# A second buffer for the raw up-projection weights of a two-layer encoder, and a new placement of its SBUF buffers

## What is computed

```python
def conv_ffn(h, w_up, conv_w, conv_b, w_down):
    u = h @ w_up                                   # 1024 -> 2 * 2816
    y = conv_b
    for j in range(CONV_WIDTH):                    # causal depthwise, width 3
        y = y + conv_w[j] * _shift(u, CONV_WIDTH - 1 - j)
    a, g = jnp.split(y, 2, axis=-1)
    return (jax.nn.silu(g) * a) @ w_down           # 2816 -> 1024
...
    h = h + m @ w_out[i]
    h = h + conv_ffn(rmsnorm(h, ffn_norm_g[i]), w_up[i], conv_w[i], conv_b[i], w_down[i])
```

## Time and profile before

| | us |
|---|---|
| median of 3 runs | 2754.95 |
| lowest, highest | 2752.99, 2756.72 |
| the profiled execution | 2758.29 |
| its span, first to last recorded instruction | 2756.5 |

### The profile page before, as it was taken

The page is one execution under the profiler, slowest core; times in us unless marked ns, Lnnn a source line. Parts: engine busy times, 40 slices in busy tenths (PEclk is TensorE's granted clock), DMA queues, the critical chain, the costliest instruction groups (busy, mean ns, idle before and its releaser), DMA issues. The chain is left out here.

```text
span 2756.5 us, 40721 instructions
## 1 busy us (share of the span) xinstructions
PE 2610.5 (95%) x14038; PEld 2265.8 (82%) x14038; DVE 1557.0 (56%) x2684; ACT 1267.7 (46%) x2809; POOL 1512.9 (55%) x1083
## 2 busy tenths in 40 slices
PE   7799899999879999999899999999988999999999
PEld 6599788888668888888789999989866888888877
DVE  5899777741755565555541114656238555555645
ACT  5687666641433333333345546767224333333332
POOL 2034433203667777767755443555138776777773
PEclk9899999999899999999999999999989999999999
DMA  5100000101011121111131111333101111111212
GB/s 177 46 24 24 28 9 6 69 24 39 31 38 54 49 67 51 46 46 61 46 119 47 50 43 28 87 90 108 63 31 41 51 46 46 52 55 49 65 38 92
DMA packets 77352, 147.16 MB, mean 53 GB/s; under 512 B 8528, under 2 KB 45568, under 8 KB 75552
## 3 DMA queue, kind: packets, MB, share of 16 engines
q1 hardware_dynamic: 77216, 145.38, 16.1%
HBM read 122.22 MB, written 13.69 MB: 49 GB/s over the span
## 5 line engine op out<-in xcount | busy, mean ns | idle before, releaser
L729 PE MATMUL banks<-XQH,WH 128*128 128x512 f32 x1120 | 441.9, 395 | 41.3 <-ACT U L450 26.4
L594 POOL TENSOR_TENSOR WL<-WR,WH 128x512 fp32r<-128x512 f32 x216 | 379.0, 1774 | 185.7 <-ACT WH L430 169.0
L729 PE MATMUL banks<-XQH,WL 128*128 128x512 f32 x1120 | 438.6, 392 | 0.0
L729 PE MATMUL banks<-XQL,WH 128*128 128x512 f32 x1120 | 438.5, 391 | 0.0
L855 DVE TENSOR_TENSOR XT<-XT,banks 128x1024 f32<-128x1024 f32 x176 | 214.3, 1218 | 180.6 <-PE banks L764 180.5
L729 PEld LDWEIGHTS banks<-XQH,WH 128*128 128x128 f32 x1120 | 212.0, 189 | 95.7 <-issue 29.9
L594 POOL TENSOR_TENSOR WL<-WF,WH 128x512 fp32r<-128x512 f32 x168 | 256.4, 1537 | 5.2 <-ACT WH L436 5.2
L729 PEld LDWEIGHTS banks<-XQL,WH 128*128 128x128 f32 x1120 | 211.9, 189 | 44.8
L729 PEld LDWEIGHTS banks<-XQH,WL 128*128 128x128 f32 x1120 | 212.2, 189 | 43.1
L839 DVE SCALAR_TENSOR_TENSOR YG<-U,CONVW,YG 128x1023 f32<-128x1023 f32 x88 | 170.1, 1933 | 95.9 <-ACT YG L474 95.8
L764 PE MATMUL banks<-AH,WH 128*128 128x512 f32 x640 | 197.6, 390 | 2.6 <-DVE XT L855 2.6
(11 more groups left out here) (326 smaller groups left out, 6577.3 us busy)
## 6 DMA issues: line engine op xcount, KB each, us to landing
WR<-in_up SPq DMA_DIRECT2D x88, 512.0 KB, 4.2
WF<-in_down SPq DMA_DIRECT2D x88, 256.0 KB, 2.6
HT<-HC SPq DMA_DIRECT2D x224, 64.0 KB, 2.0
QWR<-in_qkv SPq DMA_DIRECT2D x8, 1536.0 KB, 7.5
XT<-in_xT SPq DMA_DIRECT2D x16, 512.0 KB, 7.8
OWR<-in_w_o SPq DMA_DIRECT2D x16, 512.0 KB, 3.3
QWR1F<-in_qkv SPq DMA_DIRECT2D x4, 1536.0 KB, 6.3
spill<-XT SPq DMA_DIRECT2D x8, 512.0 KB, 11.2
```

The source lines that it names most:

```text
L594: pool.tensor_tensor(out_, src, hi.bitcast(F32), ALU.subtract).then_inc(signal, 1)
L729: mm = pe.matmul(BANK[bank], w[:, n, b * P:(b + 1) * P], x[:, b, :], start=(first and b == 0 and w is WH and x is XH[i]), stop=(b == 3 and ...
```

## The change

Two things are changed.

1. **Two raw buffers.** Even pairs are loaded into WR, odd pairs into a new tile `RAW_ODD` (WRB), each with its own semaphore. Pair p now waits for the low parts of pair p - 2. The first odd load waits until PE has summed the squares of the norm (`norm.summed`), since WRB takes the place of `ACC`, which that sum reads. SP's order changes: pairs 1, 2 and 3 are issued ahead of the loop, and in the loop the down weights come first, then pairs 4 and 5 (numbers of the first turn). ACT's wait ahead of `bias(pair, 0)` of pair 20 becomes a wait for pair 20's own low parts.
2. **Placement.** To find 8 KB, large buffers start at 384 modulo 512 bytes in place of 0, so that nothing is lost ahead of the first one; ROOTS, BITF and IDB share one row of 512 bytes that is later reused; CONVW and CONVB are packed; VAR lies in the last 64 bytes. Built, the buffers up to GAIN lie 128 bytes lower than before, those of the feed-forward part 640 bytes lower, ACC and QKVB 384 bytes higher. So all large buffers keep their distances modulo 512. WRB starts at 221056, WR at 102272, also equal modulo 512.

```diff
+PLACE = 384
...
     def row(self):
-        self.at = (self.at + ROW - 1) // ROW * ROW
+        self.at = (self.at - PLACE + ROW - 1) // ROW * ROW + PLACE
...
+    def landed(self):
+        return self.at(16, 32 * ((self.p + 1) // 2))
...
+        VAR = nc.alloc_sbuf_tensor_at(f"VAR{stage}", [P, TT], F32, offset=c.top - 64)
...
-        VAR = m.take(f"VAR{stage}", [P, TT], F32)
+        RAW_ODD = nc.alloc_sbuf_tensor_at(f"WRB{layer}", [P, 2, D], F32, offset=m.at)
...
-                sp.wait_ge(w_lo, CLASSIC if p == 1 else Pair(it, p - 1).end())
+                if p >= 2:
+                    sp.wait_ge(w_lo, CLASSIC * (p - 1) if p < 4 and it is None else Pair(it, p - 2).end())
                 for k in range(2):
-                    sp.dma_start(RAW[:, k, :], up[pair.tap(k)]).then_inc(raw_landed, 16)
+                    sp.dma_start((RAW, RAW_ODD)[p % 2][:, k, :], up[pair.tap(k)]).then_inc(raw_landed[p % 2], 16)
...
+            sp.wait_ge(norm.summed, 1)
             load_pair(None, 1)
+            load_pair(None, 2)
+            load_pair(None, 3)
             with sp.Fori(0, LOOPS) as it:
-                load_pair(it, 2)
                 load_down(it, 0)
-                load_pair(it, 3)
-            load_pair(None, LAST - 1)
-            load_pair(None, LAST)
+                load_pair(it, 4)
+                load_pair(it, 5)
...
-            act.wait_ge(w_lo, last.end())
+            act.wait_ge(w_lo, pair.end())
...
+        c.IDB = nc.alloc_sbuf_tensor_at("IDB", [P, P], BF16, offset=m.at)
+        c.ROOTS = nc.alloc_sbuf_tensor_at("ROOTS", [P, TT * DSA.nh], F32, offset=m.at + 2 * P)
+        c.BITF = nc.alloc_sbuf_tensor_at("BITF", [P, 17], F32, offset=m.at + 2 * P + roots)
```

More of the change, by code:

```diff
@@ L311, in ffn_phase @@
         AH = m.take(f"AH{layer}", [P, 2, S], F32R)
[L312 removed]
+        RAW_ODD = nc.alloc_sbuf_tensor_at(f"WRB{layer}", [P, 2, D], F32, offset=m.at)
+        m.at += 2 * 4 * D
+        assert m.at <= c.top - 64
         norm = Norm(c, stage, VAR, sem, c.bank[7], Y0[:, 0, :], c.ACC)
@@ L318, in ffn_phase @@
         uses = slot_uses()
-        raw_landed, d_landed = sem("raw_landed"), [sem(f"d_landed{d}") for d in range(DOWN)]
+        raw_landed, d_landed = [sem("raw_even"), sem("raw_odd")], [sem(f"d_landed{d}") for d in range(DOWN)]
         w_sum, w_hi, w_lo = sem("w_sum"), sem("w_hi"), sem("w_lo")
@@ L330, in ffn_phase, with quarters, classic_w @@
         block = ctx.enter_context(nc.Block())
[L332 to L338, removed]
+        def quarters(p):
+            r = (RAW, RAW_ODD)[p % 2]
+            return [r[:, k, h * HALF:(h + 1) * HALF] for k in range(2) for h in range(2)]
+        def classic_w(p, n):
+            return quarters(p)[(0, 2, 1, 3)[n]]
         def high(n):
@@ L349, in source @@
         def source(pair, k):
-            return (A11, full(pair.slot + 1), full(pair.slot + 2), S3_AT, A12, A22, S4_AT)[k]
+            a11, a12, a21, a22 = quarters(pair.p)
+            return (a11, full(pair.slot + 1), full(pair.slot + 2), a21, a12, a22, a11)[k]
         def wait_slot(eng, it, n):
@@ L425, in weights_high @@
                     if made is None:
-                        act.wait_ge(raw_landed, pair.at(32, 32 * pair.p))
+                        act.wait_ge(raw_landed[pair.j], pair.landed())
                     else:
@@ L597, in classic_low @@
                 for n in range(CLASSIC):
-                    subtract(low(CLASSIC * p + n), CLASSIC * p + n + 1, CLASSIC_W[n], high(CLASSIC * p + n), w_lo, w_hi)
+                    subtract(low(CLASSIC * p + n), CLASSIC * p + n + 1, classic_w(p, n), high(CLASSIC * p + n), w_lo, w_hi)
             def weights_low(pair, *which):
@@ L613, in first_sums @@
             def first_sums(pair):
-                pool.wait_ge(raw_landed, pair.at(32, 32 * pair.p))
+                a11, _, a21, a22 = quarters(pair.p)
+                pool.wait_ge(raw_landed[pair.j], pair.landed())
                 wait_slot(pool, pair.it, pair.slot + 1)
-                sum_of(pair, full(pair.slot + 1), A21, A22, ALU.add)
+                sum_of(pair, full(pair.slot + 1), a21, a22, ALU.add)
                 pool.wait_ge(w_sum, pair.sums(1))
-                sum_of(pair, S3_AT, A11, A21, ALU.subtract)
+                sum_of(pair, a21, a11, a21, ALU.subtract)
             def second_sums(pair):
+                a11, a12, a21, a22 = quarters(pair.p)
                 wait_slot(pool, pair.it, pair.slot + 2)
                 pool.wait_ge(w_sum, pair.sums(2))
-                sum_of(pair, full(pair.slot + 2), A22, S3_AT, ALU.subtract)
+                sum_of(pair, full(pair.slot + 2), a22, a21, ALU.subtract)
                 pool.wait_ge(w_sum, pair.sums(3))
                 pool.wait_ge(w_lo, pair.slots(1))
-                sum_of(pair, S4_AT, A12, full(pair.slot + 2), ALU.subtract)
+                sum_of(pair, a11, a12, full(pair.slot + 2), ALU.subtract)
             def x_low(q):
@@ L2762, in program @@
         roots = 4 * TT * DSA.nh
-        c.NHALF, c.ROOTS = small("NHALF", TT * DSA.nh, low), small("ROOTS", TT * DSA.nh, low + roots)
-        c.RSTD, c.HGAIN = small("RSTD", TT, low + 2 * roots), small("HGAIN", 4, low + 2 * roots + 4 * TT)
-        low += 2 * roots + 4 * TT + 16
-        top = nc.sbuf_usable_end // ROW * ROW
-        m = Map(nc, (low + ROW - 1) // ROW * ROW, top - 2 * 4 * S)
+        c.NHALF = small("NHALF", TT * DSA.nh, low)
+        c.RSTD, c.HGAIN = small("RSTD", TT, low + roots), small("HGAIN", 4, low + roots + 4 * TT)
+        low += roots + 4 * TT + 16
+        top = (nc.sbuf_usable_end - PLACE) // ROW * ROW + PLACE
+        m = Map(nc, low, top - 2 * 4 * S)
+        m.row()
         low_tiles = 4 * DB * S // (4 * PROJ)
```

17 lines of the change are left out of this document (9 added, 8 removed).

## The result

| | before | after |
|---|---|---|
| median (4 runs each), us | 2755.84 | 2738.78 |
| lowest, highest | 2752.99, 2756.89 | 2734.65, 2740.06 |
| span of the profiled execution | 2756.5 | 2737.1 |

The ratio is 0.9937, 95% interval 0.992 to 0.9954. Forecast were 2739 us and a range of 2732 to 2748. The median agrees almost exactly, and that is partly luck: several terms of the sum were off in both directions, as will be seen, and the parts of the program that nothing touches differ by several microseconds from one execution to the next.

The account below looks back on a forecast made before the run. PE, busy 95% of the span, was taken as the bound. Each phase saves 4.36 + 2.10 + 0.3 = 6.8 us, two phases 13.6, plus 2.3 at the start: 15.9 off 2754.95 gives 2739 us, range 2732 to 2748.

Parts of the forecast that it names:

- What bounds the kernel: Whole kernel: PE is busy 95% of the span; only its own waits count, not ACT's 81.6 us for raw weights.
- The stop ahead of pair 21: End of each feed-forward phase: PE's wait for ACT's second copy falls from 6.38 to about 2.0 us, 4.36 us saved.
- The 1.08 us: End of phase: POOL's first low part of pair 21 waits until DVE's gate ends, shifting the chain 4.36 instead of 5.44 us.
- The clock: Pair 21's matmuls, after PE's stop: PE's low granted clock cost 2.10 us a phase, taken as saved.
- rival 1: After the 2.0 us stop the clock falls anyway, costing 2.10 us in each phase: 2743 us; chance 0.22.
- L823: End of phase: of PE's 0.93 us wait for DVE, 0.6 to 0.7 stays; 0.3 us a phase counted as saved.
- The start: Start of phase and first loop turn: hardly any gain; 2.3 us taken, between 0 and 2.6.
- the 13.2 us: PE's wait for ACT's copies at the start of each phase (L450): it stays, nothing counted.
- the residual add: PE's three waits for DVE, 2.6 us in the two phases: pair 3's earlier load saves 2.3 us.
- The placement: Buffer addresses: large buffers keep their distances modulo 512, so only the absolute start could matter; 0 us taken.
- The bound of 1%: Placement ceiling from DVE's rows: matmuls off a 512-byte line 1% longer would cost 32 us, giving 2771 us; chance 0.07.
- SP's queue: Loads in the loop: down loads now precede both pair loads; no new wait stands in front of the down loads.

Follow-up runs that it names:

- e3_all_but_last: Changed kernel with every pair but 21 loaded early; pair 21's load and YALT's bias wait as before the change: 2749.92 us, ratio 0.9981.
- e2_only_last: Changed kernel with only pair 21 loaded early; pairs 2 to 20 wait and stand in SP's queue as before the change: 2745.15 us, ratio 0.9959.
- e4_yalt_wait: Changed kernel with one line undone: ACT's wait ahead of YALT's bias is again for pair 21's low parts: 2745.13 us, ratio 0.9963.
- j_tail: Changed kernel with ACT's second copy for pair 20 ahead of pair 21's high parts 2 and 3, and DVE's c22 ahead of pair 20's gate: 2733.75 us, ratio 0.992.
- g_start: Changed kernel with pair 2's first high part ahead of T2's high parts, and ACT's last pair 1 copies ahead of pair 2's third high part: 2734.41 us, ratio 0.9922.
- i_start2: Changed kernel with pair 2's first high part ahead of T2's, and ACT's copies and pair 2's high parts 2 and 3 ahead of pair 0's silu: 2736.99 us, ratio 0.9932.
- f_copy_first: Changed kernel with ACT's second copy for pair 20 moved ahead of pair 21's high parts 2 and 3: 2738.8 us, ratio 0.9938.
- h_both: Changed kernel with the moves of f_copy_first and g_start together: 2734.18 us, ratio 0.9931.

## Why the prediction was right, and where it was not

**What bounds the kernel: right.** Of ACT's 81.6 us of waiting for raw loads some 14 belong to pair 21 in the two phases, and they held most of the gain. The other 67 were worth 4.5 us of PE time (`e3_all_but_last` against before) to 9.1 (`e2_only_last` against the changed kernel). To count them as a gain would have been wrong by a factor of 7 to 15.

**The stop ahead of pair 21: right, to the decimal.** Saved were 4.45 us (6.44 to 1.99) in layer 0 and 4.36 us (6.38 to 2.02) in layer 1; forecast 4.36. The 1.08 us that POOL would lose beside DVE's gate were 1.01. The rule of the Trainium skill (SBUF — State Buffer, section "Who interferes with whom"), by which a DVE instruction with two SBUF inputs contends with a GpSimd instruction that reads SBUF, agrees with these 1.01 us.

**The clock: half right.** The term of 2.10 us a phase was taken as saved in both. In the profile after, pair 21 took 1353.51 - 1334.20 = 19.31 us in layer 0, almost the 19.18 us of full speed, and 2689.07 - 2668.22 = 20.85 in layer 1. So the saving was some 1.8 us in layer 0 and 0.3 in layer 1. The term is a little large to begin with: it ends pair 21 at 2708.74, where the chain's piece starts, but the first matmul of `lower` started at 2708.58, so the low clock cost 1.94 us and not 2.10. And rival 1 read rows 8 as a clock already going down two microseconds into the stop; a mean of 0.80 from 2682 to 2684 with levels of 1.00 and 0.50 puts the fall at 2683.2, three microseconds into it. The larger error is in the form: the case was put as one yes or no for both phases, with 0.22 for no. But it comes out anew in each phase of each execution: it fell in 2 of 6 phases of the three profiles of the changed kernel, and in 4 of all 14 phases of the study with such a stop. By these the term should have been about 1.4 us in a phase (10 of 14 times 1.8, 4 of 14 times 0.3).

**L823: the size was wrong, and the mechanism underrated.** Saved was the whole 0.93 us in either phase, not 0.3. The step that failed is DVE's schedule, worked out at 2699.2 against 2698.5 with every tap slowed for a whole POOL instruction. In layer 0, where the clock held as the schedule assumes, the two YALT taps took 3.52 us together and not 4.6, the gate 2.12 and not 1.7, and DVE was just in time: L836 ended at 1349.91 + 0.69 = 1350.60 and PE went on at 1350.65 without idle time.

```profile
1343.53 3.52 DVE L852 SCALAR_TENSOR_TENSOR YALT<-U,CONVW,YALT 128x1023 f32<-128x1023 f32 x2
1347.15 2.12 DVE L859 TENSOR_TENSOR YALT<-YALT,YG 128x1024 f32<-128x1024 f32 x1
1349.91 0.69 DVE L836 TENSOR_TENSOR U<-banks,U 128x512 f32<-128x512 f32 x1
```

With the old wait it was late by 0.92 us where the clock had fallen and by 2.53 where it had held (`e4_yalt_wait`). The prediction weighed only the wait of before, 0.93; it did not ask what the old wait would cost once PE comes earlier.

**The start: as said for the 13.2 us, too small for the loop.** The stop at L450 stayed (13.24, 13.25). The waits for the residual add went (2.6 us; 2.3 were forecast). Not forecast were 0.8 us in layer 0 and 1.3 in layer 1 more: 0.65 and 0.3 in the first down-projection beyond its recorded waits, 0.1 and 0.3 in the eight others, and in layer 1 0.7 in two pairs of products (see `e3_all_but_last`).

**The placement: right.** 1.0007 (0.9996 to 1.0018) with everything else undone. The bound of 1% taken from DVE's rows was far too wide for PE: the upper end of the interval, 0.18%, is 5 us.

**SP's queue: right.** No load stands in front of PE in the changed kernel.

In sum: the forecast of the two long pieces was 15.9 us and the profile has 17.5. Against the first profile: stop 8.8 for 8.7, clock 2.1 for 4.2, L823 1.9 for 0.6, residual add 2.6 for 2.3, the rest 2.1 for 0. The errors nearly cancel.

## What to carry to other kernels

A second buffer is worth what the engine that bounds the kernel waits for, not what the reader of the buffer waits for: 82 us of waiting held some 17 us, and more than half of that at one seam, the last item of a loop, where PE ran out of work before the late load was through. Where two items share a buffer, look for the second, quieter wait that guards the same memory: loosening it was one line and gave 1.1 us in one phase and 2.6 in the other. And when a stop is removed, ask which instruction in a fixed order is next by a microsecond or two. Here it took two moves on two engines at once (`j_tail`); the first alone gave nothing, and a microsecond of what both gave went to the wait behind it.

## What the runs showed of the hardware

**A stop of 2.0 us is on the edge for TensorE's clock.** All profiles of the study with such a stop ahead of pair 21 are counted here (the three of the changed kernel, `e2_only_last`, `e4_yalt_wait`, `g_start`, `i_start2`). After 14 stops of 1.99 to 2.04 us the granted clock fell to 0.50 in four and stayed at 1.00 in ten, at the same place of the program. Of four stops of 2.17 to 2.20 us (`f_copy_first`, `h_both`) three were followed by a fall and one was not. After the stops of 0.7 to 1.3 us among products and down-projections it stayed. A fall after a 2 us stop made the long piece 1.5 to 1.9 us longer.

**DVE was slower where POOL had no idle time.** Eight DVE subtractions of 128x512 took 4.89 us in the kernel before, where POOL was idle beside them for 2.2 us, and 11.43 us in `g_start`, where it worked beside them for all but 1.8 us. The whole stretch of DVE's work there grew from 25.2 to 31.2 us. That fits the small gain from an earlier start of POOL, and `i_start2`, where ACT's copies no longer hold PE up, waits for DVE instead.
